# Leaving two products of the last three pairs to the end, LayerNorm 2 beside them, bf16 weights in row blocks

## What is computed

```python
    y = jnp.concatenate([rms_norm(ya, g_mix_a), rms_norm(yb, g_mix_b)], axis=-1).astype(x.dtype)
    return jnp.einsum('bse,ed->bsd', y, w_out)

def swiglu(x, w_up, w_down):
    gate, up = jnp.split(jnp.einsum('bsd,df->bsf', x, w_up), 2, axis=-1)
    return jnp.einsum('bsf,fd->bsd', jax.nn.silu(gate) * up, w_down)
...
    for i in range(DEPTH):
        mix = token_mixer(x, w_in[i], b_in[i], sinks[i], g_mix_a[i], g_mix_b[i], w_out[i])
        x = layer_norm(ALPHA * x + mix, ln1_g[i], ln1_b[i])
        x = layer_norm(ALPHA * x + swiglu(x, w_up[i], w_down[i]), ln2_g[i], ln2_b[i])
```

## Time and profile before

| | before |
|---|---|
| time, median of 3 runs (lowest, highest) | 3010.86 us (2981.76, 3242.6) |
| time of the profiled execution | 2991.63 us |
| its span, slowest of 8 cores (fastest) | 2990.6 us (2976.1) |
| mean granted TensorE clock of the cores | 0.981 to 0.984 |
| PE busy | 2756.5 us, 92% |
| DVE busy | 1965.6 us, 66% |
| ACT busy | 735.6 us, 25% |
| POOL busy | 554.9 us, 19% |
| moved by DMA | 400.59 MB, mean 134 GB/s |

### The profile page before, as it was taken

How to read it: one execution, slowest core, us unless ns; L and a number is a source line. 1 busy time by engine, 2 the same in 40 slices (tenths; PEclk the granted TensorE clock), 3 DMA queues, 4 the chain that set the end, 5 groups by cost and what they waited for, 6 DMA issues and landing times.

```text
span 2990.6 us, 41458 instructions; the slowest of 8 cores (2976.1 to 2990.6 us)
## 1 busy us (share of the span) xinstructions
PE 2756.5 (92%) x14966; PEld 1324.0 (44%) x15077; DVE 1965.6 (66%) x2700; ACT 735.6 (25%) x1075; POOL 554.9 (19%) x579
## 2 busy tenths in 40 slices
PE   0799999999999799989999999997899999999995
PEld 0344555444566444434444444443344444444442
DVE  0164554588788754478865566675788756666787
ACT  0000000177665424523310022211233200122114
POOL 4000000022111174711100000035200000000167
PEclk9999999999999899999999999999999999999997
DMA  9745311457665755869977745578588678544653
GB/s 158 126 94 114 87 52 50 101 113 130 134 145 121 205 164 155 225 109 152 152 129 181 178 88 91 95 155 216 138 172 171 126 173 184 112 87 89 145 128 116
DMA packets 192570, 400.59 MB, mean 134 GB/s; under 512 B 89072, under 2 KB 112752, under 8 KB 174704
## 3 DMA queue, kind: packets, MB, share of 16 engines
q0 software_dynamic: 36032, 186.43, 38.1%
q1 hardware_dynamic: 142512, 186.32, 22.1%
q10 hardware_dynamic: 13824, 25.17, 2.7%
HBM read 491.42 MB, written 97.06 MB: 197 GB/s over the span
## 4 chain that ended last, share of the span: by engine, by line
PE 78%; DMA 7%; DVE 4%; another core or an unknown queue 3%; issue 3%; ACT 2%; SPq 1%; POOL 1%; ACTq 0%; DVEq 0%; POOLq 0%
PE sp L1382 47%; PE sp L481 7%; PE sp L728 7%; PE sp L468 6%; PE sp L1194 4%; DMA z2s<-arena 4%; SPq L139 1%; DMA arena<-x1s 1%; PE sp L526 1%; PE sp L538 1%; DMA arena<-z2s 1%; PE sp L770 1%; DVE arena L1288 1%; ACT arena L358 1%
## 5 line engine op out<-in xcount | busy, mean ns | idle before, releaser
L1382 PE MATMUL sp<-arena 128*128 128x512 f16 x7408 | 1615.4, 381 | 57.8 <-DVE arena L1555 19.9
L1382 PEld LDWEIGHTS sp<-arena 128*128 128x128 f16 x7408 | 726.3, 98 | 947.5 <-issue 86.5
L1475 DVE TENSOR_TENSOR arena<-sp,arena 128x512 f32<-128x512 f32 (+1 forms) x348 | 236.9, 689 | 175.3 <-PE sp L1382 154.9
L1557 DVE TENSOR_TENSOR arena<-arena,sp 128x512 f32<-128x512 f32 x256 | 166.7, 682 | 131.1 <-PE sp L1382 102.8
L1194 PE MATMUL sp<-arena 128*128 128x512 bf16 x1003 | 224.5, 384 | 10.0 <-DMA arena<-wob 6.9
L728 PE MATMUL sp<-arena 128*128 128x512 bf16 x976 | 226.9, 381 | 5.4 <-ACT arena L358 2.3
L450 DVE TENSOR_TENSOR arena<-sp,arena 128x384 bf16<-128x384 f32 (+1 forms) x81 | 47.8, 605 | 272.5 <-PE sp L526 111.3
L481 PE MATMUL sp<-arena 128*128 128x512 bf16 x1001 | 220.1, 379 | 1.2
L139 POOL DMA_DIRECT2D arena<-wup x88 | 47.0, 535 | 840.2 <-DVE arena L1395 576.7
L1403 DVE TENSOR_TENSOR arena<-arena 128x2048 f16<-128x2048 f16 (+1 forms) x118 | 191.3, 1621 | 0.0
L468 PE MATMUL sp<-arena 128*128 128x384 bf16 (+1 forms) x1036 | 182.4, 337 | 0.4
(11 more groups left out here) (131 smaller groups left out, 2474.5 us busy)
## 6 DMA issues: line engine op xcount, KB each, us to landing
arena<-wup POOLq DMA_DIRECT2D x88, 1024.0 KB, 10.0
arena<-wdn POOLq DMA_DIRECT2D x32, 1408.0 KB, 14.7
z2s<-arena SPq DMA_DIRECT2D x48, 512.0 KB, 12.2
arena<-xres SPq DMA_DIRECT2D x32, 512.0 KB, 7.6
arena<-wob SPq DMA_DIRECT2D x32, 512.0 KB, 6.8
x1s<-arena ACTq DMA_DIRECT2D x64, 256.0 KB, 6.4
arena<-x1s SPq DMA_DIRECT2D x32, 512.0 KB, 7.3
arena<-z2s SPq DMA_DIRECT2D x32, 512.0 KB, 9.0
```

The source lines that it names most:

```text
L1382: ins = nc.tensor.matmul(bank(k, bk), w, x, start=(first and i == 0), stop=(last and i == len(ws) - 1), skip_group_check=True)
L1475: S_.dve(lambda: nc.vector.tensor_tensor(out=o, in0=a, in1=b, op=op), [ba, bb], [bo])
L1557: S_.dve(lambda: nc.vector.tensor_tensor(out=v, in0=v, in1=o, op=op), [b, bo], [b])
```

## The change

Nothing is computed that was not computed before; what changes is the order, places, transfers and two types:

- **Phase 1.** The narrow `wv` loads get a buffer of their own, `bwvb`, on which only products that use these columns wait. `x` is laid out so that each chunk is 128 rows of 2 KB. The two rope tables that `load_ra` loads are recorded behind the stores of tile 0 and of tile 1.
- **Phase 2.** The two `out_norm` rows of a unit move ahead of the unit's last product with V. The partial sums drained by `run(dveq, ...)` go four at a time from unit 26 on. On SP `wob` comes ahead of `xres` and of the second half's `ys`.
- **Feed-forward, first step.** `x_sums` and `u_sums` are interleaved, the first of them goes into the time of the raw products, ahead of `finish`; the two LayerNorm jobs of this step go to later steps.
- **Down stages.** The places of `x1s` and `z2s` are a ring of five chunks; the first chunk of a pair is stored after product 7, the second at the end. `x1h` is loaded on ACT's queue.
- **Weights.** `wup` and `wdn` are cast to bf16 instead of f16 and lie in memory as four blocks of columns, so that rows are 4 KB (2 KB in SBUF) and 5.6 KB (2.8 KB). Weight sums are still f16.
- **The last stage.** For pairs 5 to 7 a new function, `last_pairs`, computes products 5, 2, 4, 1, 7 first; products 3 and 6 of the three pairs follow at the end. Column half 0 is complete before them, so its LayerNorm 2 runs beside them. Behind them come the statistics of half 1 and the rest.
- **LayerNorm 2 of the first half** uses a ring of seven places instead of six.

The core of the diff:

```diff
-    k.xT_d = ein("xT", [8, 128, KC, 512])
+    k.xT_d = ein("xT", [8, KC, 128, 512])
...
-    k.wup_d = ein("wup", [FC, 128, KC, 256])
-    k.wdn_d = ein("wdn", [KC // 2, 2, 128, 2, NJ, 256])
+    k.wup_d = ein("wup", [FC, 4, 128, KC * 64])
+    k.wdn_d = ein("wdn", [KC // 2, 2, 4, 128, FG * 64])
...
+    bwvb = Buf("wvb")
...
     for q in range(4):
         S_.dma("pool", wv[:, 4 * q:4 * q + 4, 1024:1152], k.wv_d[4 * q:4 * q + 4, :, 1024:1152].rearrange("c p n -> p c n"), [], [], "wvb",
-               joins=bwv[4 * q:4 * q + 4])
+               joins=[bwvb])
...
-            S_.pe(mm, bx[t] + bwv, [k.bBK[bk]])
+            S_.pe(mm, bx[t] + bwv + ([bwvb] if c1 > 1024 else []), [k.bBK[bk]])
...
-    load_ra(0)
-    load_ra(1)
...
+    load_ra(0)
...
+    load_ra(1)
...
-                run(dveq, 2)
+                run(dveq, 2 if u < 26 else 4)
+            if p_ == 2 and u >= 27:
+                for a in k.norms[:2]:
+                    out_norm(k, *a)
+                k.norms = k.norms[2:]
...
-        if u >= 27:
-            for a in k.norms[:2]:
-                out_norm(k, *a)
-            k.norms = k.norms[2:]
...
-    for n in range(3):
-        load_xr(k, n)
-    for c in KCB + KCA[:6]:
-        y_load(k, 1, c)
...
-    for st in range(2):
-        y_load(k, st, 6)
+    y_load(k, 0, 6)
...
+            k.wlist += [(("u", st, f), k.wup_d[f].rearrange("q p n -> p q n"), KC * 256, KC, BF16, U_OFF[f % FG % 3]) for f in range(g * FG, (g + 1) * FG)]
+            k.wlist += [(("d", st, g, p), k.wdn_d[p, g].rearrange("q p n -> p q n"), FG * 256, FG, BF16, D_OFF[p])
...
     wfill(k)
+    for n in range(3):
+        load_xr(k, n)
+    for c in KCB + KCA[:7]:
+        y_load(k, 1, c)
...
-            k.S.dma("pool", v, src, [], [b], "ws")
+            k.S.dma("pool", view(k, p, n, dty).rearrange("p (q m) -> p q m", q=4), src, [], [b], "ws")
...
-        S_.dma("sp", xall[:, b, :, :], k.x1h_d[b], [bx1h[(n, hh)] for n in range(8 * kh, 8 * kh + 8)],
+        S_.dma("act", xall[:, b, :, :], k.x1h_d[b], [bx1h[(n, hh)] for n in range(8 * kh, 8 * kh + 8)],
...
+        def half_sum(p, o):
+            w, bw = k.wts["d", st, g, p]
+            v = view(k, SUMS + o, NJ * 128, F16).rearrange("p (a b) -> p a b", a=NJ)
+            b = S_.buf("wS%d" % p, SUMS + o, SUMS + o + NJ * 256)
+            S_.dve(lambda: nc.vector.tensor_tensor(out=v, in0=w[:, 0:NJ, 0:128], in1=w[:, 0:NJ, 128:256], op=ALU.subtract), [bw], [b])
+            halls[p, "6"] = ([v[:, c, :] for c in range(NJ)], b)
...
+        for p in (5, 6, 7):
+            s = 4 * (p % 2)
+            BA, BB, BD, BC = range(s, s + 4)
+            if p < 7:
+                q[p + 1] = load_xq(p + 1)
+            q11, q12, q21, q22 = q[p]
+            prod(p, "5", BB, True, p == 5)
+            prod(p, "2", BC, True, p == 5)
+            acc(q11, BB, ALU.subtract)
+            if p == 5:
+                acc(q12, BB)
+            else:
+                acc(q22, BB, ALU.subtract)
+            prod(p, "4", BA, True, False)
+            acc(q21, BC)
+            if p == 5:
+                acc(q22, BC, ALU.subtract)
+            if p < 7:
+                d_sums(st, g, p + 1, "P")
+            prod(p, "1", BD, True, True)
+            acc(q21, BA)
+            stats(ss, 0, *q21)
+            prod(p, "7", BA, False, True)
+            acc(q11, BD)
+            acc(q22, BD)
+            if p < 7:
+                d_sums(st, g, p + 1, "Q")
+            else:
+                half_sum(5, 0)
+                half_sum(6, 2816)
+            acc(q11, BA)
+            if p < 7:
+                stats(ss, 0, *q11)
+                d_sums(st, g, p + 1, "R")
+        stats_dve(0, *q[7][0])()
...
+        dv = [(0, n) for n in range(13)] + [(1, n) for n in range(11)]
+        pl = [(0, n) for n in range(13, 16)] + [(1, n) for n in range(11, 16)]
+        lnq = [lambda e=e: sub(*e) for e in dv[0:4]] + [lambda e=e: mul(*e) for e in dv[0:4]]
+        for i in range(4, 24, 2):
+            lnq += [lambda e=e: sub(*e) for e in dv[i:i + 2]] + [lambda e=e: mul(*e) for e in dv[i:i + 2]]
+
+        def ln(n):
+            for _ in range(n):
+                lnq.pop(0)()
+        for i, (p, m, bk) in enumerate(((5, "3", 0), (5, "6", 2), (6, "3", 1), (6, "6", 3), (7, "3", 5), (7, "6", 7))):
+            q11, q12, q21, q22 = q[p]
+            prod(p, m, bk, p == 5, True)
+            if m == "3":
+                acc(q12, bk)
+                acc(q22, bk)
+                stats(ss, 1, *q12)
+                if i == 0:
+                    sums_out(0)
+                    ln(2)
+                    rstd(0)
+                ln(2)
+            else:
+                acc(q22, bk, ALU.subtract)
+                if p < 7:
+                    stats(ss, 1, *q22)
+                    ln(3)
+                else:
+                    tail = stats_dve(1, *q22)
+                    ln(1)
+                    tail()
...
+        sums_out(1)
+        ln(3)
+        rstd(1)
+        pend = None
+        while lnq:
+            t = pool_tile(*pl.pop(0)) if pl else None
+            ln(min(4, len(lnq)))
+            if pend:
+                pend()
...
-                    o = zslots[4 * p + i] if last else wslot(6 - 4 * (p % 2) + i)
+                    o = zslots[4 * p + i] if last else wslot((n + 3) % 5 * 2 + hh)
...
+                            x_sums(((G3, B21, B11, ALU.subtract),))
+                            u_sums(st, f + 1, "P")
                             while fins:
                                 fins.pop(0)()
...
-                    x_sums(((G3, B21, B11, ALU.subtract), (G0, B11, B22, ALU.add), (G2, B12, B22, ALU.subtract)))
-                    for wh in "PQR":
-                        u_sums(st, f + 1, wh)
+                    x_sums(((G0, B11, B22, ALU.add),))
+                    u_sums(st, f + 1, "Q")
+                    x_sums(((G2, B12, B22, ALU.subtract),))
+                    u_sums(st, f + 1, "R")
...
-                    run_jobs(2)
-                    run_acts()
...
-            for p in range(KC // 2):
+            for p in range(5 if last else KC // 2):
...
+                def store(i, p=p, xq=xq):
+                    n = 2 * p + i
+                    bz = [Buf("z2s") for _ in range(2)]
+                    bz2s[(st, n, 0)], bz2s[(st, n, 1)] = bz
+                    S_.dma("sp", k.z2s_d[n, :, st * TS:(st + 1) * TS], view(k, wslot((n + 3) % 5 * 2), 1024, F32),
+                           [xq[2 * i][1], xq[2 * i + 1][1]], bz, "z2o")
...
+                if not last:
+                    store(0)
...
-                    for i in range(2):
-                        n = 2 * p + i
-                        o = wslot(6 - 4 * (p % 2) + 2 * i)
-                        bz = [Buf("z2s") for _ in range(2)]
-                        bz2s[(st, n, 0)], bz2s[(st, n, 1)] = bz
-                        S_.dma("sp", k.z2s_d[n, :, st * TS:(st + 1) * TS], view(k, o, 1024, F32), [xq[2 * i][1], xq[2 * i + 1][1]], bz, "z2o")
+                    store(1)
...
+                    last_pairs(st, ss, zr, xq, load_xq, acc, bh)
...
-                    z, bz = slot("zl%d" % idx, HB + NJ * 7168 - (1 + idx % 6) * 2048)
+                    z, bz = slot("zl%d" % idx, ([HB + NJ * 7168 - (1 + i) * 2048 for i in range(3)] + [wslot(i) for i in (8, 9, 6, 7)])[idx % 7])
```

117 lines of the change are left out of this document (76 added, 41 removed).

## The result

The changed kernel takes 2864.88 us (median of 4 runs, 2859.56 to 2963.68); the four runs of the kernel before now reach from 2981.76 to 3242.6 and have a median of 3053.62. In some executions the cores of one die run at a lower granted clock and take longer, so kernels are compared by their undisturbed runs, and stages by medians over cores. By these the ratio is 0.9555, with a 95% interval of 0.9442 to 0.9669, and 0.958 (0.956 to 0.9601) when the same kernel was run once more: it is faster, by 4.5 and 4.2%. The profiled execution went from 2991.6 to 2862.8 us, its span from 2990.6 to 2861.7: 128.8 us less, where 146.4 were forecast.

The account below looks back on a forecast made before the run. PE, busy 92% of 2990.6 us, bounds the kernel; only idle and lower-clock time can go. Gains 70 + 12.5 + 14.9 + 31 + 14 + 4 = 146.4 give 2844, with 1.0 more 2845 us; range 2830 to 2858 (0.60).

Parts of the forecast that it names:

- rival 2: Down stages bound by the DMAs, not the ring: gain 10 instead of 31, clock 8 instead of 14; 2872 us, chance 0.15.
- The start: First tile: products wait for their own two loads alone, no longer for the narrow wv load; gain 70 us, bounds 54 to 72.
- bursts at half clock: Rival 1: the first tile runs at half clock, in bursts of 1.7 us between loads; 2856 us, chance 0.10.
- Sixteen groups at half clock: Other bound of the start: groups of 3.4 us each would end at 64.7 us, a gain of 59.
- The layout of x: Start: 2 KB rows of x cost nothing that shows; tile 1's last part lands at 65.6 us, needed at 66.3.
- The end of the attention: Last attention units and output start: wob wait of 6.86 us goes, norm rows give 5.6; gain 12.5, bounds 7 and 14.
- The two starts of the feed-forward: First step of both halves: moved LayerNorm jobs and earlier sums close PE gaps of 7.43 and 7.45; gain 14.9, bounds 9 and 17.
- The down stages: Ring of five lets x1s and z2s loads go earlier, x1h leaves SP; gain 31 of 37.5 us, bounds 10 and 35.
- Taking turns: Down stages: if DMA engines alternate queues by packet, all waits would go and the sum be 4 us shorter.
- The clock: PE's 31.84 us at half clock, half of it lost, goes with the gaps; gain 14 us, bounds 5 and 16.
- bf16: Feed-forward weight sums from bf16 to f16 run as fast as from f16; 0 us.
- The end: Tail behind the last feed-forward product, 41.4 us, becomes about 36 plus 2; gain 4, bounds -5 and 12.

Follow-up runs that it names:

- e2: The changed kernel with the narrow wv loads again writers of the sixteen wide buffers; span 2931.1 us, 69.4 more.
- e12: The changed kernel with x laid out as before the change, in long rows; ratio 0.9569 to the kernel before, first feed-forward product at 1187.2 us instead of 1174.0.
- e9: The changed kernel with norm rows at the unit's end and partial sums two at a time; first output product at 947.6 us against 940.8.
- e7: The changed kernel with the raw step's two activation sums and first weight sum behind finish again; ratio 0.9485 to the kernel before, raw step 23.8 us in both.
- e3: The changed kernel with feed-forward weights in whole rows again, still bf16; ratio 0.9689 to the kernel before, three down stages 450.4 us against 421.6.
- e14: The changed kernel with whole weight rows and the old ring with both stores at a pair's end; ratio 0.9653 to the kernel before, three down stages 444.3 us.
- e10: The changed kernel without the four 1 MB x1h loads in the second down stage; that stage 138.6 us against 148.1, ratio 0.9433 to the kernel before.
- e6: The changed kernel with f16 instead of bf16 feed-forward weights, still in row blocks; ratio 0.9511 to the kernel before, every stage within 2 us.

## Why the prediction was right or wrong

The measured 2864.88 us lies outside the forecast of 2830 to 2858, on the slow side, and inside the wider 2815 to 2888. From profile to profile the gain was 128.8 us, not 146.4. What is missing is mostly one term, the waits of the down stages; it came out between the forecast of 2845 and rival 2's 2872.

- **The start**, forecast 70 (54 to 72), measured 72.1, and 69 when it alone was undone (e2). The named waits were the right thing to read, and the clock of the earlier trace rows was the right evidence against bursts at half clock. (Sixteen groups at half clock would end at 64.4, not 64.7; the bound of 59 stays.)
- **The layout of x** was costed at nothing because the last part of tile 1 comes in time. That holds, but it was the wrong place to look. Without the layout 13 us of the start are given back (e12), through stores of K that I had not followed: PE came to their products 70 us earlier than before, while `x` tiles were still loading. That the start gained what was forecast was luck as far as this goes: the layout made good a loss that the forecast did not see.
- **The end of the attention**, forecast 12.5 (7 to 14), measured 15.4 on the profiled core and 13.8 in the median. The norm rows and the partial sums together make 6.7 (e9), where 5.6 were forecast for the norm rows, and the 6.86 us for `wob` are gone.
- **The two starts of the feed-forward**, forecast 14.9 and a share of the clock, measured 17.3 to 19.8. The waits of the earlier trace rows went. The reason was half right: the early sums brought none of it (e7), which leaves the LayerNorm jobs that were taken out of the step and the interleaving of the sums (neither was run by itself). And at the first step two new waits came, 2.62 us for `wup` and 3.54 for GpSimd.
- **The down stages are the step that failed.** PE's waits there were to fall by 31 of 37.5 us; they fell by 16.1, to 21.4 (4.9, 13.6 and 2.9 in the three stages). With the clock the stages gained 22.3 on the profiled core (25.2 in the median). The step read the wait in the earlier trace rows as one of order, a load behind a store in its place, and gave all of it to the ring. The ring alone is worth nothing (e3 against e14: 450.4 and 444.3). What the step did not ask is what an early load meets: weight loads in rows of 11 KB, behind which the longest `x1s` load took 28.4 us, about as long as the store and the load of the earlier trace rows together. The row blocks, which I put down as hidden in the up steps and left out of this term, are half of the pair. And they are paid for: shorter rows took the DMAs from 0.85 to 0.96 of the second stage, DVE now waits for weights as well, and 9.5 us of that stage are the transfers of `x1h` (e10). The sign that I had named, DVE waits for `x1s` and `z2s` under 5 us, failed with 6.1 and 6.8. This was rival 2, with 10 and 8 us; it came in a milder form.
- **Taking turns.** From the Trainium skill's rule that a DMA engine changes queue packet by packet (DMA: Bandwidth & Descriptors, Queues, rings and completion order) I took that all waits would go. The direction was right, the longest waits got shorter; but the DMAs ran full, for which the 0.85 of the earlier trace rows was the row.
- **The clock**, forecast 14: PE's busy time fell by 10.8. The earlier trace rows were seven of the stretches at half clock; all twelve in which PE worked held 50.7 us of its busy time, and 25.9 are left in the changed kernel.
- **bf16**, forecast 0, is 0 (e6): L1395 takes 1217 ns for 128x2048, and 1215 in the earlier trace rows.
- **The end**, forecast 4 (-5 to 12), is 0.4. The part behind the last product is 34.8 us where I had 36 and 2; but the stage grew by 6.2, and I had only counted PE's two sums in it. The wait of 3.95 for a DVE row stretched by GpSimd was visible before as a long L1403 row and I did not price it.
